# Sixteen of twenty-four blocks of a short convolution's input projection as Strassen quads

## The reference

```
def conv_mixer(h, w_in, w_conv, w_out):
    b_gate, c_gate, xv = jnp.split(h @ w_in, 3, axis=-1)
    return (b_gate * short_conv(c_gate * xv, w_conv)) @ w_out

def short_conv(u, w):      # width 3, one filter per feature, along the tokens
    return lax.conv_general_dilated(u, w[:, None, :].astype(u.dtype), window_strides=(1,),
        padding=[(CONV_WIDTH // 2, CONV_WIDTH // 2)],
        dimension_numbers=('NWC', 'WIO', 'NWC'), feature_group_count=u.shape[-1])

sh1, sc1, g1, sh2, sc2, g2 = ...   # from c @ ada_w
hx = hx + g1 * conv_mixer(modulate_2(rms_norm(hx, norm_mix[1]), sh1, sc1), w_in, w_conv, w_out)
```

## Time and profile before

| | us |
|---|---|
| median of 3 runs | 2272.05 |
| lowest and highest | 2271.41, 2272.97 |
| span of the profiled execution | 2270.2 |
| three first blocks in halves | 1726.03 to 1734.96 |
| the other 21 blocks | 1734.96 to 1849.35 |

### The profile page before, as it was taken

The page is one execution under the profiler, slowest core; times in us unless marked ns, Lnnn a source line. Parts: engine busy times, 40 slices in busy tenths (PEclk is TensorE's granted clock), DMA queues, the critical chain, the costliest instruction groups (busy, mean ns, idle before and its releaser), DMA issues.

```text
span 2270.2 us, 30637 instructions
## 1 busy us (share of the span) xinstructions
PE 2252.1 (99%) x10984; PEld 1885.9 (83%) x10984; DVE 1407.1 (62%) x2155; ACT 828.0 (36%) x1175; POOL 167.8 (7%) x97
## 2 busy tenths in 40 slices
PE   9999999999999999999999999999999999999998
PEld 4888888888888898888888878888888889888887
DVE  5558766689999876755647477565436446333322
...
GB/s 314 158 130 75 63 62 179 149 75 102 92 108 147 218 67 164 76 121 75 134 96 108 96 78 211 192 191 194 133 102 75 106 98 75 111 92 95 99 93 75
DMA packets 74073, 273.94 MB, mean 121 GB/s; under 512 B 8192, under 2 KB 9088, under 8 KB 72832
## 3 DMA queue, kind: packets, MB, share of 16 engines
...
## 4 chain that ended last, share of the span: by engine, by line
PE 94%; DVE 3%; issue 1%; ACT 1%; DMA 1%; SPq 0%; DVEq 0%
PE bank L451 90%; PE bank L1250 1%; DMA res<-in_x 1%; DVE rstd L635 1%; DVE hx_lo L647 1%; PE bank L1332 0%; PE bank L1108 0%; DVE tnorm L641 0%; PE bank L1305 0%; ACT hx_hi L582 0%; DVE w_lo L410 0%; PE bank L1274 0%; DVE std L476 0%; DVE rt L2470 0%; PE bank L1247 0%
## 5 line engine op out<-in xcount | busy, mean ns | idle before, releaser
L451 PE MATMUL bank<-hx_hi,w_hi 128*128 128x512 f32 (+1 forms) x1936 | 733.5, 379 | 5.7 <-DVE hx_lo L647 4.9
L451 PE MATMUL bank<-hx_hi,w_lo 128*128 128x512 f32 (+1 forms) x1936 | 723.0, 373 | 0.0
L451 PE MATMUL bank<-hx_lo,w_hi 128*128 128x512 f32 (+1 forms) x1936 | 723.0, 373 | 0.0
L410 DVE TENSOR_TENSOR w_lo<-w_raw,w_hi 128x1024 fp32r<-128x1024 f32 x305 | 373.2, 1224 | 415.9 <-ACT w_hi L402 409.4
L402 ACT ACTIVATE w_hi<-w_raw 128x1024 fp32r<-128x1024 f32 x350 | 369.1, 1055 | 392.1 <-PE bank L451 338.4
L451 PEld LDWEIGHTS bank<-hx_hi,w_hi 128*128 128x128 f32 x1936 | 364.7, 188 | 73.6 <-issue 4.9
L451 PEld LDWEIGHTS bank<-hx_hi,w_lo 128*128 128x128 f32 x1936 | 364.4, 188 | 64.8
L451 PEld LDWEIGHTS bank<-hx_lo,w_hi 128*128 128x128 f32 x1936 | 364.7, 188 | 63.5 <-issue 1.4
L2399 DVE SCALAR_TENSOR_TENSOR bank<-zpad,cols,bank 128x512 f32<-128x512 f32 x352 | 232.1, 746 | 4.7 <-ACT bank L1827 4.6
L451 PE MATMUL bank<-hid_hi,w_hi 128*128 128x512 f32 (+1 forms) x594 | 218.5, 368 | 0.0
L451 PE MATMUL bank<-hid_hi,w_lo 128*128 128x512 f32 (+1 forms) x594 | 217.2, 366 | 0.0
...
## 6 DMA issues: line engine op xcount, KB each, us to landing
w_raw<-in_wstream SPq DMA_DIRECT2D x350, 512.0 KB, 3.7
ada_raw<-in_ada_nk ACTq DMA_DIRECT2D x128, 512.0 KB, 3.9
...
ada_w<-in_ada_kn SPq DMA_DIRECT2D x6, 512.0 KB, 7.1
...
crow<-in_crow SPq DMA_DIRECT2D x3, 512.0 KB, 8.2
```

What stands on the lines that cost most here:

```text
L410: nc.vector.tensor_tensor(w_lo[nb.at % RING][:], w_raw[nb.at % RAW][:], w_hi[nb.at % RING][:].bitcast(F32), ALU.subtract).then_inc(lo_read ...
L451: ins = nc.tensor.matmul(out_ap, s, m, start=first and at == 0, stop=last and at == n - 1)
```

## The change

Blocks of output tiles 0 and 1 and two of the three of tile 7 stay plain. The other 16 are taken in 8 pairs ("quads"), each a product with 2 x 2 quarters on either side: on the weights' side the pair's two blocks by the even and the odd input tiles, on the activations' side the even and the odd input tiles by the two halves of 256 tokens. `CIN_QUADS` lists them: ("b", u) holds the b_gate blocks of tiles u and u + 1, ("c", u) the c_gate and xv blocks of tile u, for u = 2, 4, 6 (with ("c", u + 1) but for the last).

A quad is seven quarter products of 4 steps x 3 matmuls x 256 columns (Strassen's scheme in Winograd's form), into three banks, with two sets of banks. Four of the seven take sums of weight quarters (`qsum`), which GpSimd makes from the raw megabyte of the quad (`qraw`, one DMA each); ScalarE and VectorE split four pieces (`quad_hi`, `quad_lo`). Four take sums of input tiles, made once: VectorE norms whole tiles again (`cin_norm`), GpSimd makes four sums for each of 4 pairs of tiles (`combined_pool`), ScalarE and VectorE split them (`t_hi`, `t_lo`). The products are put together by two copies of ScalarE and four additions of VectorE, which read a PSUM bank and an SBUF tile: `quad_mid_dve`, `quad_inner_dve` (two), `quad_outer_dve`. The last product adds onto the first one's bank and waits for `quad_mid`.

The diff, cut to its core (ScalarE's and VectorE's new order is in the listings behind it; the buffers and the host's rearranging of the weights are left out):

```diff
+CIN_QUADS = []
+for _u in (2, 4, 6):
+    CIN_QUADS += [("b", _u), ("c", _u)] + ([("c", _u + 1)] if _u < 6 else [])
+N_QUADS = len(CIN_QUADS)
...
+        def quad_sums_pool(pool, g):
+            w11, w12, w21, w22 = (qraw[g % 2][:, n * QUARTER:(n + 1) * QUARTER] for n in range(4))
+            s1, s2, s3, s4 = (qsum[n // 2][:, n % 2, :] for n in range(4))
+            pool.wait_ge(q_landed[g % 2], OPENED + 16 * (g // 2 + 1))
+            if g >= 1:
+                pool.wait_ge(q_lo, OPENED + 4 * (g - 1) + 2)
+            nc.gpsimd.tensor_tensor(s1, w21, w22, ALU.add).then_inc(q_sum, 1)
+            pool.wait_ge(q_sum, OPENED + 4 * g + 1)
+            nc.gpsimd.tensor_tensor(s2, s1, w11, ALU.subtract).then_inc(q_sum, 1)
+            if g >= 1:
+                pool.wait_ge(q_lo, OPENED + 4 * (g - 1) + 3)
+            nc.gpsimd.tensor_tensor(s3, w11, w21, ALU.subtract).then_inc(q_sum, 1)
+            pool.wait_ge(q_sum, OPENED + 4 * g + 2)
+            nc.gpsimd.tensor_tensor(s4, w12, s2, ALU.subtract).then_inc(q_sum, 1)
...
+        def quad_pe(pe, g, taken):
+            bank_a, bank_b, bank_c = q_banks[g % 2]
...
+            for at, (n, x, dst, half, opens) in enumerate((
+                    (0, x11, bank_a, 0, True), (3, t2, bank_a, 1, False), (2, t1, bank_b, 0, True),
+                    (4, t3, bank_b, 1, False), (5, x22, bank_c, 0, True), (6, t4, bank_c, 1, False),
+                    (1, x21, bank_a, 0, False))):
+                if at in (0, 1, 3, 5):
+                    pe.wait_ge(q_lo, OPENED + 4 * g + (1, 2, None, 3, None, 4)[at])
...
+                elif at == 6:
+                    pe.wait_ge(q_mid, OPENED + g + 1)
...
+                for j in range(KT // 2):
+                    if g == 0 and n in (2, 3, 4, 6):
+                        pe.wait_ge(t_lo_ready, OPENED + j + 1)
...
-            for u in range(1, KT):
-                for kind in range(3):
-                    block_pe(pe, *cin_job(u, kind))
+            for kind in range(3):
+                block_pe(pe, *cin_job(1, kind))
...
+            for g in range(N_QUADS):
+                quad_pe(pe, g, first_taken if g < 2 else none)
+            pe.wait_ge(q_post, OPENED + 3 * (N_QUADS - 2) + 2)
+            block_pe(pe, Block(B_CIN + 6), bx[0])
+            pe.wait_ge(q_post, OPENED + 3 * N_QUADS)
+            block_pe(pe, Block(B_CIN + 7), by[1])
+            pe.wait_ge(q_out, OPENED + N_QUADS)
...
+            for g, (kind, u) in enumerate(CIN_QUADS):
+                y = (qy_b[u // 2 % 2] if kind == "b" else qy_c[u % 2])
+                late = CIN_QUADS[g - 1][1] if g >= 1 and CIN_QUADS[g - 1][0] == "c" else None
+                if g + 1 < N_QUADS:
+                    quad_lo(dve, g + 1, 0)
+                if late is not None:
+                    mixed(late)
+                quad_mid_dve(dve, g, y)
+                if late is not None:
                     for t in range(3):
...
+                        mixed_tap(late, t)
+                    mixed_gate(late)
+                if g + 1 < N_QUADS:
+                    quad_lo(dve, g + 1, 1)
+                quad_inner_dve(dve, g, y)
+                if g + 1 < N_QUADS:
+                    quad_lo(dve, g + 1, 2)
+                quad_outer_dve(dve, g, y)
+                if g + 1 < N_QUADS:
+                    quad_lo(dve, g + 1, 3)
...
+            split_lo(dve, Block(B_CIN + 3))
+            split_lo(dve, Block(B_CIN + 4))
+            mixed_whole(6)
...
+            combined_pool(pool, 0)
+            combined_pool(pool, 1)
+            quad_sums_pool(pool, 0)
+            combined_pool(pool, 2)
+            combined_pool(pool, 3)
+            for g in range(1, N_QUADS):
+                quad_sums_pool(pool, g)
```

More of the change, by code:

```diff
@@ L58 @@
 B_CIN = B_SD0 + HT
-B_COUT = B_CIN + 24
+B_COUT = B_CIN + 8
 B_SW1 = B_COUT + 8
@@ L167, in program @@
         hx_lo = sb("hx_lo", [P, KT, L], F32R, r_hx + 16 * KB)
-        ada_raw = [sb(f"ada_raw{s}", [P, D]) for s in range(2)]
+        r_ada = region(8 * KB)
+        ada_raw = [sb(f"ada_raw{s}", [P, D], F32, r_ada + 4 * KB * s) for s in range(2)]
         r_crow = region(12 * KB)
@@ new lines, in combined_hi, with combined_lo @@
+        def combined_hi(act, j, shift):
+            act.wait_ge(t_sum, OPENED + 4 * j + 4)
+            for n in range(4):
+                ins = nc.scalar.activation(t_hi[:, j, n, :], t_raw[j % 2][:, n, :], *(
+                    (ACT.Copy,) if shift(j, n) is None else (ACT.Identity, shift(j, n))))
+            ins.then_inc(t_hi_ready, 1)
+        def combined_lo(dve, j, shift):
+            dve.wait_ge(t_hi_ready, OPENED + j + 1)
+            for n in range(4):
+                if shift(j, n) is None:
+                    ins = nc.vector.tensor_tensor(t_lo[:, j, n, :], t_raw[j % 2][:, n, :], t_hi[:, j, n, :].bitcast(F32),
+                                                  ALU.subtract)
+                else:
+                    ins = nc.vector.scalar_tensor_tensor(out=t_lo[:, j, n, :], in0=t_raw[j % 2][:, n, :], scalar=shift(j, n),
+                                                         in1=t_hi[:, j, n, :].bitcast(F32), op0=ALU.add, op1=ALU.subtract)
+            ins.then_inc(t_lo_ready, 1)
@@ L1988, in _ @@
             act.wait_ge(block_done, B_CIN)
[L1989 to L2002 removed]
+            cin_shift = combined_shift(80)
@@ new lines, in cin_out, with mixed_hi @@
+            def cin_out(u, kind):
+                act.wait_ge(block_done, Block(B_CIN + 3 * u + kind).count(1))
+                nc.scalar.activation((cb if kind == 0 else cc)[u % 2][:], bx[kind][:], ACT.Copy).then_inc(x_free, 1)
+            def mixed_hi(u):
+                act.wait_ge(cy_f, u + 1)
+                nc.scalar.activation(cy_hi[:, u, :], cacc[u % 2][:], ACT.Copy).then_inc(cy_h, 1)
+            cin_out(0, 0)
+            cin_out(0, 1)
+            split_hi(act, Block(B_CIN + 1))
@@ L2003, in _ @@
+            split_hi(act, Block(B_CIN + 5))
+            mixed_hi(6)
+            split_hi(act, Block(B_CIN + 6))
+            act.wait_ge(block_done, B_CIN + 7)
+            nc.scalar.activation(cc[1][:], bx[0][:], ACT.Copy).then_inc(x_free, 2)
+            split_hi(act, Block(B_CIN + 7))
+            mixed_hi(7)
             square_act(act, B_COUT, JY["cout"], nffn1)
@@ new lines, in mixed_rest, with mixed_whole @@
+            def mixed_rest(u):
+                s = u % 2
+                dve.wait_ge(cy_f, u + 1)
+                dve.wait_ge(cy_h, u + 1)
+                nc.vector.tensor_tensor(cy_lo[:, u, :], cacc[s][:], cy_hi[:, u, :].bitcast(F32), ALU.subtract)\
+                    .then_inc(cy_l, 1)
+            def mixed_whole(u):
+                mixed(u)
+                for t in range(3):
+                    mixed_tap(u, t)
+                mixed_gate(u)
+            cin_norm(0)
+            cin_norm(1)
@@ new lines, in _ @@
+            split_lo(dve, Block(B_CIN + 1))
+            cin_norm(2)
+            combined_lo(dve, 0, cin_shift)
+            split_lo(dve, Block(B_CIN + 2))
+            cin_norm(3)
+            mixed(0)
+            quad_lo(dve, 0, 0)
+            combined_lo(dve, 1, cin_shift)
+            for t in range(3):
+                mixed_tap(0, t)
+            mixed_gate(0)
+            quad_lo(dve, 0, 1)
+            combined_lo(dve, 2, cin_shift)
+            mixed_rest(0)
+            quad_lo(dve, 0, 2)
@@ L2764, in stream_blocks @@
     c_in = inputs["conv_w_in_2"][0]
-    cin = np.stack([tiles(c_in[:, n * D:(n + 1) * D]) for n in range(3)], 1).reshape(-1, P, KT, P)
+    cin = np.stack([tiles(c_in[:, n * D:(n + 1) * D]) for n in range(3)], 1)
+    quads = np.stack([np.stack([cin[u, 0], cin[u + 1, 0]] if kind == "b" else [cin[u, 1], cin[u, 2]], 1)[:, :, HALVES]
+                      for kind, u in CIN_QUADS])
+    cin = np.concatenate([cin[0], cin[1], cin[7, 1:]])
     for layer in range(2):
@@ L2830 @@
     ada_w = [inputs["ada_w"][0], inputs["ada_w_2"][0], inputs["ada_w_2"][1]]
+    blocks, quads = stream_blocks(inputs)
     arrays = {
-        "wstream": stream_blocks(inputs),
+        "wstream": blocks,
+        "qstream": quads,
         "ada_kn": ada_w[0][:, :2 * D].reshape(KT, P, 2, 2, L).transpose(3, 1, 0, 2, 4),
```

305 lines of the change are left out of this document (252 added, 53 removed).

## The result

| | median of the runs | profiled span | against before |
|---|---|---|---|
| before | 2272.35 us (2271.41 to 2272.97, 4 runs) | 2270.2 us | 1 |
| changed | 2292.11 us (2291.67 to 2292.68, 4 runs) | 2290.6 us | 1.0088 (1.0074 to 1.0102) |

The changed kernel is 19.8 us slower, where 2290 us (+17.9) was forecast. First the page of the changed kernel: busy us by engine, then three of its rows of 40 slices in tenths.

The account below looks back on a forecast made before the run. TensorE's matmuls were taken to bound the stage. Terms -6.6 + 17.1 + 6.4 + 0.7 + 0.3 = +17.9 us gave a span of 2288.1, hence a forecast of 2290 us; range 2276 to 2301, a little over 80%.

Parts of the forecast that it names:

- Matmuls, -6.6: Input projection on TensorE: 384 matmuls of 512 columns, 87.2 us, become 672 of 256 columns, 80.5 us; -6.6 us.
- The clash: Throughout the stage, VectorE instructions with two SBUF inputs and GpSimd's sums take turns, so their times add; +9 to +26, 74%.
- Rival (a): Port not contended for these instructions, only for reductions: opening costs 3.3, quads nothing; -2.3 us, 2270 us; chance 12%.
- The order of turns: At the shared port, VectorE's queued instruction goes ahead of GpSimd that asked earlier; the page's order would add 1.7 us.
- Opening, +17.1: Product 2 of quad 0: TensorE waits for the fourth combined tile, ready at 1770.9, in three waits; +17.1 us.
- rival (c): TensorE's clock falls during the opening's waits, costing up to 7.2 us more in quad 0; 2298 to 2305 us; 8%.
- The quads, +6.4: TensorE waits at product 7 of quad 0 and product 2 of quads 4, 6 and 7; +6.4 us, bounds 0 and 15.
- The last weights' split, +0.7: Behind the quads, the split for block B_CIN+6 stands behind the last quad's quad_outer: 10.8 against 10.1; +0.7 us.
- The last tile, +0.3: Last tile's chain behind the quads: a VectorE split of 1.22 replaces the wait for ScalarE's 0.63; +0.3 us.

Follow-up runs that it names:

- the halved kernel: Kernel before, with the 504 matmuls of 512 columns in its 21 later input projection blocks each made as two of 256; 2279.27 us, ratio 1.0032.
- e2_weights_blank: Changed kernel with only GpSimd's 32 sums of weights replaced by memsets that read nothing; 2277.84 us, ratio 1.0026.
- e3_tiles_blank: Changed kernel with only GpSimd's 16 sums of tiles replaced by memsets that read nothing; 2287.06 us, ratio 1.0065.

## Why the prediction was right, step by step

- **Matmuls, -6.6.** Right: -6.5 by the halved kernel's pitch. The whole skeleton without waits is 4.2 us faster and its other terms are +0.7 and +0.7, so the rows' price holds. The formula of the Trainium skill (TensorE: Matmul & The Clock Gate, section Back-to-back issue gap), which the page gives for an isolated matmul, would have made it, as an estimate, -9.5; the trace does not agree with it, 227.0 and 120.1 ns for 215.8 and 109.2.
- **The clash.** Right, and now shown, not only inferred from the earlier trace rows: take GpSimd's reads away and the splits are back at 1.22 us. The overlap at the handovers, 0.14 us, is that of the earlier trace rows too. Rival (a), 2270 us, would have needed splits of 1.22 us beside GpSimd's sums, and they took 2.10. The Trainium skill (SBUF — State Buffer, section SBUF: two separate sides) says that VectorE with two inputs in SBUF contends only with a GpSimd operation that reads SBUF. By that rule, memsets do no harm to the splits, and the trace agrees with 1.220 us.
- **The order of turns.** Wrong, and hidden by luck. I followed, where VectorE's next instruction went ahead of a GpSimd that had asked before it. In the changed kernel that did not happen once: in each of the 29 cases from 1735 to 1850 us in which a GpSimd sum had to wait and its row stands beside an unmerged row of VectorE, it waited for the VectorE instruction that ran when it asked, and VectorE's next one with two inputs in SBUF came behind it. That is the order by which my laying out gives 1772.6. I also had two of quad 1's sums ahead of the fourth tile, and all four were. Both errors should have brought the tile later than my 1770.9; less the 1.0 us of the later start it came at 1770.2. Where the laying out was too long by these 2.4 us and more is not shown, so that the term came within 1 us is in part luck.
- **Opening, +17.1.** Right in size, with the luck just told. The fourth tile came 35.3 us behind the start of the fourth block, where I had laid out 35.9 (1770.9 less 1734.96) and TensorE had use for it at 18.8, so the term is +16.4; the run without tiles puts the whole opening, with the clock behind the last wait, at 17.9 us, of which 1.0 comes back later. Its parts were not as forecast. I had three waits of 7, 4 and 6 us in product 2; the trace has 2.8 us already at the last plain block, whose split took 2.29 for 1.22 beside quad 0's weight sums, and then 3.8, 1.9 and 4.2. The rest of the 16.4, 3.8 us, are the starts behind the waits and matmuls at the 1.2 GHz level, which stand in for waiting.
- **The lower clock, rival (c).** It came, and it did not decide. I had priced it at up to 7.2 us behind the opening. The sum put it at nothing. It held for 4 us there, 2 us lost, of which 0.5 to 1.1 was paid in the end. The step that was too large is the assumption that the clock stays low for all five products that are left. The page on idle waits that throttle the engine (the Trainium skill, TensorE: Matmul & The Clock Gate, section HAM oscillation — how this bites in real kernels) is borne out by the 0.50 of those stretches.
- **The quads, +6.4.** 5.7 us in six waits. Product 2 of quads 4, 6 and 7 was forecast with 1.9, 1.3 and 2.4 us and has 0.9, 0.5 and 0.9; product 7 of quads 3, 4 and 6 waits for quad_mid with 0.3, 1.2 and 1.9, where I had seen that wait at quad 0 alone, with 0.8, and quad 0 has none. The cause is the same, an overfull VectorE; the waits stand one step earlier.
- **The last weights' split, +0.7.** 0.7 (1858.25 us, 0.57 of idle time by the trace).
- **The last tile, +0.3.** The old wait for cy_lo is gone, but I overlooked that the output projection's first product now needs both counts of y_free, which come with the last cpad product: 1.2 for 0.5, so +0.7.
- **The sum.** In the trace -6.5 + 16.4 + 2.0 (the clock behind the last wait) + 5.7 + 0.7 + 0.7 = +19.0, and +1.0 by which this execution's stage started later: 20.0 of the 20.4 us between the spans. Some 0.4 us stays unassigned. Against the forecast the terms moved by +0.1, -0.7, +2.0, -0.7, 0 and +0.4, so their errors partly cancel.

The sizes that I expected for the two halves of the clash, before e2_weights_blank and e3_tiles_blank ran, were wrong (9 and 9, measured 14.3 and 5.1). The prediction had them in one term and didn't depend on it.
